# The first expert query from X unscaled: norm and shift applied at the scores, query weights in other homes, and a re-cut tail

## What is computed

```
x  = x + g1 * (mixed @ w_out)
h2 = rms_norm(x, norm2_g) * (1 + sc2) + sh2
q  = (h2 @ wq) as [token, 8 heads, 2 halves, 128]
s  = q . keys          # 128 scores for each head and half
top_s, top_i = top 16 of each half; best 16 of the 16 x 16 sums
idx = i1 * 128 + i2;  g = softmax(best)
out = sum over 8 x 16 of  g * gelu(u_tab[idx] . h2) * v_tab[idx]
x  = rms_norm(x + g2 * out, norm_f_g)
```

## Time and profile before

| what | value |
|---|---|
| median of 3 runs | 1889.62 us (1889.24 to 1889.65) |
| the profiled execution | 1890.34 us, of which the span is 1888.4 us |
| busy in the span | PE 93%, DVE 71%, ACT 45%, POOL 16% |
| HBM traffic | 508.67 MB, mean 269 GB/s |
| the chain that ended last | PE 67%, DMA 20%, DVE 9%, ACT 3% |

### The profile page before, as it was taken

One profiled execution on the slowest core, in us unless ns is written; L12 is line 12 of the kernel. 1 busy time (PEld: TensorE's weight loads), 2 busy tenths in 40 slices (PEclk: granted clock), 3 DMA queues, 4 the chain that ended last, 5 costly groups with the idle time before them and its releaser, 6 DMA issues.

```text
span 1888.4 us, 26541 instructions
## 1 busy us (share of the span) xinstructions
PE 1764.2 (93%) x10490; PEld 1389.7 (74%) x10490; DVE 1341.4 (71%) x2636; ACT 848.4 (45%) x1628; POOL 304.8 (16%) x341
## 2 busy tenths in 40 slices
PE   8999999999999999999999999999999787777776
PEld 8999997999999999979999899865555333322222
DVE  7676678777676766787777698887775567575745
ACT  6344557543353335575343664545443233332323
POOL 0000112000000002210000000033454333433330
PEclk9999999999999999999999999999999998999999
DMA  9676552667557755437675442699999999999997
GB/s 322 205 243 204 174 182 90 209 237 260 175 191 243 253 178 169 163 109 248 214 244 172 96 134 96 232 392 416 411 420 422 421 421 422 421 421 421 421 422 300
DMA packets 197765, 508.67 MB, mean 269 GB/s; under 512 B 10419, under 2 KB 143879, under 8 KB 161032
## 3 DMA queue, kind: packets, MB, share of 16 engines
q1 hardware_dynamic: 160488, 238.51, 38.0%
q0 software_dynamic: 37152, 268.45, 34.3%
HBM read 505.87 MB, written 1.06 MB: 268 GB/s over the span
## 4 chain that ended last, share of the span: by engine, by line
PE 67%; DMA 20%; DVE 9%; ACT 3%; issue 1%; POOL 0%; SPq 0%; DVEq 0%; ACTq 0%
PE PB L322 13%; PE PB L323 12%; PE PB L324 12%; DMA BIG<-in_c_experts,BIG 11%; PE PB L2828 8%; PE PB L635 4%; PE PB L637 4%; PE PB L636 4%; DMA HTF<-in_c_experts,BIG 4%; DMA HIF<-in_c_experts,BIG 2%; DMA RAW<-in_c_experts,BIG 2%; PE PB L2754 2%; DVE LOWS L280 1%; DVE BIG L3096 1%; DMA RAW<-in_ffn_w_up 1%
## 5 line engine op out<-in xcount | busy, mean ns | idle before, releaser
L280 DVE TENSOR_TENSOR LOWS<-RAW,HIGH 128x2048 fp32r<-128x2048 f32 (+2 forms) x130 | 298.8, 2306 | 41.6 <-ACT HIGH L268 41.0
L322 PE MATMUL PB<-HTR,HIGH 128*128 128x256 f32 (+1 forms) x1072 | 306.4, 286 | 0.6 <-DVE LOWS L300 0.4
L323 PE MATMUL PB<-HTR,HIGH 128*128 128x256 f32 (+1 forms) x1072 | 305.5, 285 | 0.0
L324 PE MATMUL PB<-HTR,LOWS 128*128 128x256 f32 (+1 forms) x1072 | 304.7, 284 | 0.0
L268 ACT ACTIVATE HIGH<-RAW 128x2048 fp32r<-128x2048 f32 (+3 forms) x138 | 264.7, 1923 | 75.6 <-DMA RAW<-in_ffn_w_gate 32.0
L322 PEld LDWEIGHTS PB<-HTR,HIGH 128*128 128x128 f32 x1072 | 202.7, 189 | 5.9 <-DVE LOWS L280 0.7
L323 PEld LDWEIGHTS PB<-HTR,HIGH 128*128 128x128 f32 x1072 | 200.9, 187 | 4.4
L324 PEld LDWEIGHTS PB<-HTR,LOWS 128*128 128x128 f32 x1072 | 201.1, 188 | 2.2
L3188 ACT ACTIVATE BIG<-BIG 128x2 f32<-128x2 f32 (+1 forms) x162 | 32.7, 202 | 361.8 <-DVE BIG L3096 361.7
L2828 PE MATMUL PB<-HIF,BIG 128*128 128x512 f32 x340 | 163.8, 610 | 32.7 <-ACT BIG L3199 32.7
L2828 PE MATMUL PB<-RAW,BIG 128*128 128x512 f32 x340 | 161.1, 601 | 27.7 <-ACT BIG L3199 27.6
(11 more groups left out here) (485 smaller groups left out, 3990.6 us busy)
## 6 DMA issues: line engine op xcount, KB each, us to landing
RAW<-in_ffn_w_up SPq DMA_DIRECT2D x32, 1024.0 KB, 6.6
RAW<-in_ffn_w_down SPq DMA_DIRECT2D x32, 1024.0 KB, 5.1
RAW<-in_ffn_w_gate SPq DMA_DIRECT2D x31, 1024.0 KB, 5.6
RAW<-in_w_in SPq DMA_DIRECT2D x22, 1120.0 KB, 5.7
RAW<-in_c_wmod SPq DMA_DIRECT2D x20, 1024.0 KB, 4.8
BIG<-in_ffn_w_gate SPq DMA_DIRECT2D x12, 1024.0 KB, 6.2
BIG<-in_ffn_w_up SPq DMA_DIRECT2D x12, 1024.0 KB, 9.0
BIG<-in_ffn_w_down SPq DMA_DIRECT2D x12, 1024.0 KB, 4.9
```

The costliest lines, as they stand in the source:

```text
L280: e.tensor_tensor(u.l, u.raw, u.h.bitcast(F32), ALU.subtract).then_inc(*low_done.up())
L322: e.matmul(o, lh, rh, start=k == 0, stop=False)
L323: e.matmul(o, lh, rl, start=False, stop=False)
L324: last = e.matmul(o, ll, rh, start=False, stop=k == len(ls) - 1)
```

## The change

VectorE makes the low halves of block 0 ahead of the means of block 1 and does all four X updates of block 0 in one go. The query of head 0 and block 0 is made from X itself: TensorE transposes each chunk of X as soon as it is updated (`raw_turn`), ScalarE copies it out times the gain (`RAWT`), and `raw_query` multiplies by the weights. The reciprocal root of the mean square is applied by VectorE as it reads the scores from PSUM, together with the shift's own score, `SHIFTED`. That is (shift @ wq) . keys: ScalarE multiplies half of the weights by the shift and GpSimd the other half, GpSimd adds them up, and TensorE sums over partitions and multiplies by the keys. The squares of X move from ScalarE to one VectorE operation with an accumulator. The normed block is still transposed and shifted, for the dot products and later queries, but behind the scores; block 1's first X update and VectorE's shifts stand behind the first eight indices.

Query weights get other homes: heads 0 and 1 in CTXF, 2 in HTF, 6 alone goes through a slot, 7 in ROW_B. With it the first places are eight, all in slots, the four places in HTF come free behind head 2 in the place of head 1, SyncE's order is another, and gathers 0, 2, 4 and 6 wait for block 1's products. `XAT` is rounded down to a multiple of 16 floats: 9504, byte 38016.

At the end, batches are single from gather 240 on, VectorE adds the second halves of the last two v rows and TensorE the first, the very last v row comes in two quarter rows, block 1's first half is added and squared in two pieces, and the last product with the gain is shared with GpSimd.

```diff
-        XAT = BIGN - 2 * SLOT * 2
+        XAT = (BIGN - 2 * SLOT * 2) // 16 * 16
...
-            got["wq"] = [plan(query_source(j), (8, 256), query_done.at(j + 4), 1, split=False, slots=NS if j == 2 else NS - 1)
-                         for j in (2, 6)]
+            got["wq"] = [plan(query_source(6), (8, 256), query_done.at(8), 1, split=False, slots=NS)]
...
             gate(1)
+            lower(0)
             means(1)
-            lower(0)
             scale(1)
             low_half(e, SECOND["out"][3], 1)
             e.wait_ge(mixer_in.sem, 192)
-            mix_update(e, 0, 0)
-            lower(1)
-            for j in range(1, 4):
+            for j in range(4):
                 mix_update(e, 0, j)
             first_norm_vector(e)
-            mix_update(e, 1, 0)
...
+            e.wait_ge(WQ_IN[0].sem, WQ_AT[0])
+            for k in range(4):
+                x = e.activation(SHIFT_PARTS[:, k, :].rearrange("p (c n) -> p c n", c=2), WQ[0][:, k, :, :], ACT.Copy,
+                                 scale=GA[:, 5, k:k + 1])
+            x.then_inc(*shift_done.up())
             square(1)
             raise_(0)
             sqrt_scalar(e, R8[:, 12:16])
-            raise_(1)
+
+            def raw(*ks):
+                for k in ks:
+                    if k % 2 == 0:
+                        e.wait_ge(turned.sem, TURNED - 3 + k // 2)
+                    e.activation(RAWT[:, k, :], raw_of(k), ACT.Copy, scale=GA[:, 4, k:k + 1]).then_inc(*h2_s.up())
+
+            def shift_copy(dst, bank):
+                e.wait_ge(*shift_full.next())
+                e.activation(dst, PB[bank][:, 0:256].rearrange("p (c n) -> p c n", c=2), ACT.Copy).then_inc(*shift_done.up())
+
+            raw(0, 1, 2, 3)
+            shift_copy(SHIFT_WIDE, 6)
+            raw(4, 5)
+            shift_copy(SHIFTED, 7)
+            raise_(1, lambda: raw(6))
...
+                part(0, j, 4, 8).then_inc(*out_done.up())
+                raw_turn(e, j - 1)
+                if j == 2:
+                    e.wait_ge(oo_done.sem, 3)
+                    e.wait_ge(squares.sem, 5)
+                    e.wait_ge(p_step.sem, SHIFT_SUMMED)
+                    for c in range(2):
+                        x = e.matmul(PB[6][:, c * 128:(c + 1) * 128], SHIFT_SUM[:, c, :], ONES[:, :], start=True, stop=True)
+                    x.then_inc(*shift_full.up())
+            e.wait_ge(keys_in.sem, 16)
+            e.wait_ge(shift_done.sem, SHIFTS_BEFORE + 2)
+            for c in range(2):
+                x = e.matmul(PB[7][:, c * 128:(c + 1) * 128], SHIFT_WIDE[:, c, :], KEYT[:, c, :], start=True, stop=True)
+            x.then_inc(*shift_full.up())
+            raw_query(e, 0, 4)
+            e.wait_ge(h2_s.sem, 6)
+            gla_turn(1)
+            raw_turn(e, 3)
+            raw_query(e, 4, 8)
...
+        def raw_turn(e, j):
+            if j == 0:
+                e.wait_ge(ot_low.sem, OT_BEFORE + 4)
+            elif j == 2:
+                e.wait_ge(h2_s.sem, 2)
+            elif j == 3:
+                e.wait_ge(shift_done.sem, SHIFTS_BEFORE + 3)
+            e.wait_ge(x_done.sem, X_MIX + j + 1)
+            for k in (2 * j, 2 * j + 1):
+                x = e.transpose(raw_of(k), X[:, 0, k * 128:(k + 1) * 128], IDENT)
+            x.then_inc(*turned.up())
+
+        def raw_query(e, first, end):
+            for k in range(first, end):
+                if k < 7:
+                    e.wait_ge(h2_s.sem, k + 1)
                 else:
-                    if j == 3:
-                        tile_ready(e, SECOND["out"][j])
-                    part(0, j, 4, 8).then_inc(*out_done.up())
-            e.wait_ge(ot_low.sem, OT_BEFORE + 8)
-            e.wait_ge(x_done.sem, X_MIX + 3)
-            mix_second(e, 0)
+                    e.wait_ge(h2_v.sem, 1)
+                for c in range(2):
+                    x = e.matmul(PB[c][:, 0:128], WQ[0][:, k, c, :], RAWT[:, k, :], start=k == 0, stop=k == 7)
+                    if k == 7:
+                        x.then_inc(*query_done.up())
...
-        PLACES = [ROW_B] + SLOTS[1] + SLOTS[2] + SLOTS[3]
+        assert [t.slot for t in SECOND["wq"]] == [4]
+
+
+        PLACES = SLOTS[0] + SLOTS[1] + SLOTS[2] + SLOTS[3]
         EARLY = len(PLACES)
-        HOMES = {2: SLOTS[4][0], 3: SLOTS[4][1], 4: WQ2, 5: ROW_A, 6: SLOTS[0][0], 7: SLOTS[0][1]}
+        HOMES = {6: SLOTS[4][0], 3: SLOTS[4][1], 4: WQ2, 5: ROW_A, 7: ROW_B}
...
+        PLACE_BEHIND = {0: [], 1: []}
+        for j in (2, 3, 5, 6, 7):
+            behind = [HTF[:, i:i + 2048] for i in range(0, 8192, 2048)] if j == 2 else [HOMES[j]]
...
-        BATCHES = [(g,) for g in range(64)] + [(g, g + 1) for g in range(64, 252, 2)] + [(g,) for g in range(252, 256)]
+        BATCHES = [(g,) for g in range(64)] + [(g, g + 1) for g in range(64, 240, 2)] + [(g,) for g in range(240, 256)]
...
+            e.wait_ge(x_done.sem, X_MIX + 3)
+            second_part(e, 0, 0, 2)
             scores(0)
+            second_part(e, 0, 2, 4)
+            e.wait_ge(ot_low.sem, OT_BEFORE + 8)
+            second_part(e, 0, 4, 8).then_inc(*out_done.up())
+            turn_first()
...
+                    for g, v in LAST_V.items():
+                        if g == 254:
+                            e.wait_ge(row_in[PLACE_OF[v]].sem, 16 * VISIT[v])
+                            e.wait_ge(diagonal.sem, 255)
+                            e.wait_ge(row_mixed.sem, 254)
+                        else:
+                            e.wait_ge(row_in[PLACE_OF[v]].sem, 16 * VISIT[v])
+                            e.wait_ge(diagonal.sem, 256)
+                        e.scalar_tensor_tensor(PB[5][:, :], PLACES[PLACE_OF[v]][:, 1536:2048], AV[:, 1, g - 128:g - 127],
+                                               PB[5][:, :], ALU.mult, ALU.add).then_inc(*v_step.up())
+                        e.wait_ge(*v_step.last())
...
+            e.wait_ge(shift_done.sem, SHIFTS_BEFORE + 3)
+            for x in range(2):
+                e.wait_ge(*score_full.next())
+                e.scalar_tensor_tensor(src[x], PB[6 + x][:, 0:128], RSTD[:, 0:1], SHIFTED[:, x, :], ALU.mult,
+                                       ALU.add).then_inc(*score_read.up())
...
+            mix_update(e, 1, 0)
+            first_turned()
...
+                            parts = ((512, 1024, 19), (0, 256, 18), (256, 512, 20)) if b else ((0, 512, 16), (512, 1024, 17))
...
+            e.wait_ge(WQ_IN[0].sem, WQ_AT[0])
+            e.wait_ge(carry_read.sem, 8)
+            e.tensor_tensor(SHIFT_PARTS[:, 4:8, :], CTXF[:, 12:16, :], GA[:, 5, 4:8].unsqueeze(2).broadcast_to([128, 4, 256]),
+                            ALU.mult).then_inc(*p_step.up())
+            e.wait_ge(shift_done.sem, SHIFTS_BEFORE + 1)
+            for n in (4, 2, 1):
+                e.wait_ge(*p_step.last())
+                e.tensor_tensor(SHIFT_PARTS[:, 0:n, :], SHIFT_PARTS[:, 0:n, :], SHIFT_PARTS[:, n:2 * n, :],
+                                ALU.add).then_inc(*p_step.up())
...
-                if g in (1, 3, 5):
-                    e.wait_ge(out_done.sem, 6 + g // 2)
+                if g in (0, 2, 4, 6):
+                    e.wait_ge(out_done.sem, 5 + g // 2)
...
+            v = LAST_V[255]
+            for h in (1, 0):
+                e.wait_ge(row_mixed.sem, USED_BY[v][1] if h else freed[258][1][1])
+                e.indirect_dma_start(out=PLACES[PLACE_OF[v]][:, 1024 + h * 512:1536 + h * 512], out_offset=None,
+                                     in_=A["c_experts"].rearrange("n (t w) -> (n t) w", t=4),
+                                     in_offset=bass.IndirectOffsetOnAxis(ap=LAST_IDX[:, 4 + h:5 + h], axis=0)
+                                     ).then_inc(*row_in[PLACE_OF[v] if h else HALF_0].up())
+            e.wait_ge(dot_done.sem, 256)
+            e.wait_ge(sum_done.sem, 3)
+            e.wait_ge(copy_s.sem, 3)
+            e.tensor_tensor(LAST_Y[:, 256:512], X[:, 1, 768:1024], FNG[:, 768:1024], ALU.mult).then_inc(*last_y_done.up())
...
+            load_query(4)
+            e.wait_ge(squares.sem, 1)
+            e.wait_ge(pair_done.sem, 2)
+            load_query(1)
             e.wait_ge(carry_read.sem, 8)
+            e.dma_start(KEYT, A["c_keys"].rearrange("p (h k) -> p h k", h=16)).then_inc(*keys_in.up())
             load(SECOND["wq"][0].n + 1)
             load_query(3)
-            e.dma_start(KEYT, A["c_keys"].rearrange("p (h k) -> p h k", h=16)).then_inc(*keys_in.up())
-            load_query(4)
-            e.wait_ge(heads_turned.sem, HEADS_BEFORE + 2)
+            e.wait_ge(pair_done.sem, 6)
+            load_query(5)
+            e.wait_ge(oo_done.sem, 3)
+            load_query(7)
+            e.wait_ge(out_done.sem, 4)
+            e.wait_ge(keys_in.sem, 16)
             e.dma_start(IO16, A["c_cst2"][:, 2048:2064]).then_inc(*keys_in.up())
-            load_query(5)
-            e.wait_ge(out_done.sem, 4)
-            load_query(1)
-            load(SECOND["wq"][1].n + 1)
-            load_query(7)
+            load_query(2)
```

(4 more changed lines are left out.)

179 lines of the change are left out of this document (101 added, 78 removed).

## The result

The median is 1891.96 us over 21 runs (1889.45 to 1894.06), against 1889.52 for the kernel before over 21 (1888.06 to 1891.47): ratio 1.0015, 95% interval 1.0009 to 1.0021. The time lies inside the stated range at its upper edge; the sign is the other one. 0.15% is less than the 0.2% of the prediction, but 21 runs tell it from nothing. The profiled execution took 1891.59 us, its span is 1889.8.

The account below looks back on a forecast made before the run. DMA engines were taken as full from about 1233 us, so the end follows the first gather. -0.15 + 1.6 + 0.05 - 2.2 - 0.6 = -1.3 gave 1889.0 profiled, 1888.3 median; range 1884.6 to 1892.

Parts of the forecast that it names:

- What bounds the kernel: Gathers' stream: DMA engines full from about 1233 us for 638 us, so the end moves one for one with the first gather.
- I take 1.6, between the first two: Head of block 0: GpSimd's shift sums delay VectorE's chain by 1.6 us, between 2.1 and 1.1; bounds 0 and 4.4.
- GpSimd holds VectorE twice: Rival, head of block 0: GpSimd's first addition also precedes `scale(0)`; head 4.4 for 1.6, time 1891.1; chance 0.11.
- my case of 1.1: Head of block 0: VectorE slightly ahead, GpSimd's multiplication waits, its additions meet `scale(1)`; costs 1.1 us.
- waits for ScalarE's copies, which come late: Argument against a second hold at `scale(0)`: GpSimd's 2.36 us addition must wait for ScalarE's late copies.
- the two cases that I priced, 2.1 and 1.1: Head of block 0: GpSimd's multiplication holds VectorE's low half, 2.1 us; or it waits and its additions meet `scale(1)`, 1.1.
- The chain without disturbance: Head up to the index: rebuilt query chain ends at 1229.2 against 1229.35, a gain of 0.15 us.
- the first gather's new wait: First gather also waits for `out_done` 5, level at 1229.2; costs nothing more than 0.1 us, 0.05 in the sum.
- The offset: Feed-forward tiles from two moved weight slots: 5.53 us for 5.63, together -2.2; bounds 0 and -2.5.
- the grid of 64 bytes: Two weight slots: an offset that is no multiple of 64 B makes their tiles slower; given 0.65.
- The tail: Behind the last bytes: a half product moves to VectorE and the last square is narrower; -0.6 us, bounds 0 and -1.0.
- Places and load order: Query weights' homes, SP's queue order and the eighth first place: nothing; bound -1.8 to 0.

Follow-up runs that it names:

- adds_late: Changed kernel with GpSimd's three additions waiting for VectorE's scale of block 0; +2.34 us against the kernel before (1.0011), inconclusive by its time.
- pool_none: Changed kernel without GpSimd's four operations on the shift, half of the shift's score left out; -0.42 us against the kernel before (0.9999).
- row_b_first: Changed kernel with the shift's sums moved later, plus first gather into ROW_B and head 7's weights loaded late; -0.42 us against the kernel before (0.9997).
- sums_moved: Changed kernel, ScalarE making all eight copies, GpSimd only adding, from the first X update on; -0.19 us against the kernel before (1.0000).
- reordered: Changed kernel with shift sums moved and VectorE updating X first, GpSimd's additions waiting for the low half; -2.90 us against the kernel before (0.9986).
- before_pool: Kernel before, plus four GpSimd operations of the change's sizes, results unused; +5.17 us against the kernel before (1.0027).
- align_alone: Kernel before with only the slots' offset rounded down to byte 38016; -0.94 us against the kernel before (0.9995).
- align_tail: Kernel before with the slots' offset at 38016 and the tail's edits; -1.87 us against the kernel before (0.9990), -1.58 in a second series.

## Why the prediction was wrong

**What bounds the kernel** was right. The stream is as dense after as before, and the sum of what moves its start and its end makes the result: offset -0.9, rebuilt chain -0.5, the gather's second wait +0.66, lock +3.8, tail -0.9 (or -0.6): +2.2 to +2.5, measured +2.4. That the time still lay in the range is the range's width, not the sum: the sum is 3.7 off, of it 2.2 by the lock, 1.3 by the offset and some 0.3 by the chain with its wait.

**The step that failed is "I take 1.6, between the first two".** It alone turns the sign. The mechanism was named and its rows were right; the price was 3.8, near the upper bound of 4.4, and the rival "GpSimd holds VectorE twice" is what happened, though with both holds on `scale(0)`. VectorE's low half was ahead by 0.35 (1206.49, and 1206.84 for the multiplication), which is my case of 1.1: "the multiplication waits instead and the additions meet `scale(1)`". The multiplication did wait (2.60; 1.89 where it was ahead, in `adds_late`). But then it held the first half of `scale(0)` until 1209.72, and the addition the second half until 1212.20. Against such a second hold I put that the addition "waits for ScalarE's copies, which come late". They ended at 1208.50, and the multiplication only at 1209.44: the addition was ready behind it, 0.14 us later. I had also let the two cases that I priced, 2.1 and 1.1, exclude each other; the rows show one VectorE operation held by each operation of GpSimd. By the Trainium skill ("SBUF — State Buffer", "Who interferes with whom") the pair is an exclusive lock held for a whole instruction, and the trace agrees: 4.59 us for 0.75. What the rule would have said, 2.1 or more, was the better term.

**The chain without disturbance** I put at -0.15, with the first gather's new wait at +0.05. `pool_none` gave -0.49 and +0.66. `out_done` 5 did come "level", but not at 0.05: a gather behind both waits starts later. In the timelines of TensorE and GpSimd after, the last product for the first gather and for the third, and the third gather, which waits for a product alone:

```profile
1230.83 0.28 PE L323 MATMUL PB<-HIGH,HTR 128*128 128x256 f32 x1
1234.54 0.28 PE L323 MATMUL PB<-HIGH,HTR 128*128 128x256 f32 x1
1235.09 0.94 POOL L3368 DMA_INDIRECT RAW<-in_c_experts,BIG  x1 [0.43 <-PE PB L323]
```

The first product ends at 1231.11, as the index does (1231.06), and the gather starts 0.93 behind it; the third gather starts 0.27 behind its product. Why two waits that end together cost more than one, no run here shows; with the first gather's wait for the product gone (`row_b_first`) it starts 0.28 behind the index.

**The offset** at -2.2 was mis-sized: -0.9, and its interval holds zero by itself; the tiles say which (5.58, half of the way). (24 tiles at the 0.10 of the earlier trace rows are 2.4, not 2.2.) I gave the grid of 64 bytes 0.65, and it fell: other offsets give from nothing to 6.0. The -2.2 stood on the belief that RAW's 5.53 was the pace of an undisturbed slot.

**The tail**, -0.6, agrees with the 0.6 to 0.9 measured, as far as these can be told from noise. Places and load order at nothing were right: the stream's rate is unchanged. No run has ScalarE's copies apart.

**What the profile would show**: the stretched VectorE operation beside a 128x1024 GpSimd row came, but as the scale, not the low half; in `adds_late` it was the low half. TensorE's wait ahead of X's transposes was 0.49 here, hidden by the lock, and 1.92 in `pool_none`, as forecast. "Later than 1231" was named as a sign that the prediction is wrong.

## What to carry to other kernels

Idle time on GpSimd is not free: each operation there can hold the VectorE operation with two SBUF inputs that comes up beside it until it ends, and the next one holds the next, so such work goes where VectorE reads PSUM (the X updates in `sums_moved` kept their 0.42 beside GpSimd's additions) or where the held result is needed late. When work is taken out of a chain, ask what the next engine then waits for: the rebuilt query brought the index 0.5 us sooner (`pool_none`) until VectorE's order was changed for it, and then 2.0 (`reordered`; 19.28 for 21.31). And the place of an operand can be worth 6 us of 1890 for a reason that nobody has given here: it is a parameter to sweep.

## What the runs showed of the hardware

- The lock goes back and forth: with GpSimd's next operation starting 0.14 us behind the one before, a waiting VectorE operation still ran between them (ends at 1209.72 and 1212.20, each 0.28 behind GpSimd's). It also held a VectorE operation with one input and four columns (0.17 to 1.73 us in `before_pool`). The Trainium skill ("SBUF — State Buffer", "SBUF: two separate sides") names, beside operations with two SBUF inputs, those in a two-port mode; no run here shows which mode this one had.
- Sixteen products of one column took as long as of 128 columns (0.24 us each), and the granted clock fell behind them (0.63), as behind a wait of 3.53 us (0.50), but not behind the wide ones (1.00). Behind waits of 1.92 and 1.94 us it fell in one run of three (`sums_moved`, not `pool_none` and `row_b_first`).
- The same 48 products took from 5.32 to 5.63 us with nothing changed but the offset of the slots that hold the weights, moved by 16 to 144 bytes. The cause is open.
- The last 3 us of the stream run far below its rate: 8 to 50 GB/s in half microseconds in place of 420, in the six runs looked at in such slices (`before`, `after`, `align_alone`, both of `align_tail`, `reordered`).
